# Routing in a two-layer decoder trunk: the choice of experts split between seven tiles and the last, block counts ahead of ranks, embedding projections moved

## What is computed

```python
a = rmsnorm(h)
y = concat(norm(sgu(a)), norm(conv_module(a)), norm(attention(a)))
h = h + y @ w_o                       # the output projection
m = rmsnorm(h)
glog = m @ wg + bg                    # 4 groups
elog = m @ we + be                    # 32 experts, 8 in a group
# the best group, in it the two best experts of each token
# tokens sorted by expert, in blocks that hold one expert each
h = h + sum over the 2 experts: weight * (silu(m @ w_gate[e]) * (m @ w_up[e])) @ w_down[e]
h = h + sigmoid(rmsnorm(h) @ ple_gate) * rmsnorm(p @ ple_proj)   # p: an embedding per token
```

## Time and profile before

| | |
|---|---|
| Time, median of 3 runs | 2171.34 us (2170.77 to 2174.62) |
| The profiled execution, span | 2165.7 us |
| PE busy | 1985.7 us, 92% |
| DVE busy | 1033.4 us, 48% |
| ACT busy | 638.2 us, 29% |
| POOL busy | 374.1 us, 17% |
| Output projection loop of layer 0 | 435 to 587 us |
| Routing until the first expert transposes | 587 to 627 us |
| Expert blocks | 627 to 949 us |
| Embedding stage | 949 to 1090 us |

### The profile page before, as it was taken

How to read it: one execution, slowest core, us unless ns; L and a number is a source line. 1 busy time by engine, 2 the same in 40 slices (tenths; PEclk the granted TensorE clock), 3 DMA queues, 4 the chain that set the end, 5 groups by cost and what they waited for, 6 DMA issues and landing times.

```text
span 2165.7 us, 34769 instructions
## 1 busy us (share of the span) xinstructions
PE 1985.7 (92%) x8952; PEld 1098.1 (51%) x8952; DVE 1033.4 (48%) x2327; ACT 638.2 (29%) x1521; POOL 374.1 (17%) x542
## 2 busy tenths in 40 slices
PE   6999789999969999989979997898999699999898
PEld 3555456655535545544435554666555354445443
DVE  3489867754341111125434897676543421111353
ACT  3333365522111111132133333555221111111321
POOL 2232100021012222210022221000210122222100
PEclk9999999999979999999989998999999799999999
DMA  7011241000389999965210112410003899999522
GB/s 252 15 29 29 55 160 30 26 20 30 133 322 393 389 382 375 389 233 202 83 29 15 29 29 60 155 30 26 20 30 136 313 389 384 373 378 370 178 96 97
DMA packets 122222, 361.97 MB, mean 167 GB/s; under 512 B 18853, under 2 KB 54005, under 8 KB 105220
## 3 DMA queue, kind: packets, MB, share of 16 engines
q1 hardware_dynamic: 105028, 318.74, 40.6%
q0 software_dynamic: 14784, 33.59, 4.2%
q10 hardware_dynamic: 2304, 8.39, 0.9%
HBM read 319.50 MB, written 59.51 MB: 175 GB/s over the span
## 4 chain that ended last, share of the span: by engine, by line
PE 76%; DMA 11%; DVE 5%; issue 4%; ACT 3%; SPq 1%; DVEq 0%; POOL 0%; ACTq 0%; POOLq 0%
PE ps L1806 30%; DMA region_c<-in_moe_w_up_dram 8%; PE ps L2169 7%; PE ps L1827 4%; PE ps L1969 4%; PE ps L2165 4%; PE ps L1985 4%; PE ps L2005 4%; PE ps L2190 4%; PE ps L1775 3%; PE ps L2184 2%; DMA region_a<-in_moe_w_up_dram 2%; PE ps L2150 2%; PE ps L1901 2%; PE ps L2091 2%
## 5 line engine op out<-in xcount | busy, mean ns | idle before, releaser
L1806 PE MATMUL ps<-region_b,region_c 128*128 128x512 f32 x1024 | 448.0, 593 | 2.8 <-DVE region_c L1271 2.7
L1806 PEld LDWEIGHTS ps<-region_b,region_c 128*128 128x128 f32 x1024 | 191.7, 190 | 226.9 <-issue 226.4
L1806 PE MATMUL ps<-region_a,region_c 128*128 128x512 f32 x512 | 224.3, 592 | 0.0
L1686 DVE SCALAR_TENSOR_TENSOR region_a<-region_a,ps 128x128 f32<-128x128 f32 x66 | 23.4, 354 | 385.5 <-ACT region_a L1134 385.5
L2169 PE MATMUL ps<-region_c,region_a 128*128 128x512 f32 x336 | 148.6, 595 | 14.1 <-DMA region_c<-in_moe_w_up_dram 13.9
L1806 PEld LDWEIGHTS ps<-region_a,region_c 128*128 128x128 f32 x512 | 96.5, 190 | 117.0 <-issue 117.0
L1969 PE MATMUL ps<-region_c 96*128 96x512 f32 (+3 forms) x384 | 146.6, 491 | 0.0
L1134 ACT ACTIVATE region_a<-ps 128x128 f32<-128x128 f32 x66 | 21.8, 331 | 363.1 <-PE ps L2169 242.4
L1466 DVE TENSOR_REDUCE neg_max<-ps 128x1 f32<-128x128 f32 (+7 forms) x128 | 96.9, 757 | 50.7 <-PE ps L1976 47.4
L1985 PE MATMUL ps<-ident,region_a 128*128 128x128 f32 x576 | 91.0, 285 | 26.5 <-ACT region_a L1066 25.0
L2169 PEld LDWEIGHTS ps<-region_c,region_a 128*128 128x128 f32 x336 | 62.1, 190 | 93.6 <-issue 93.6
(11 more groups left out here) (352 smaller groups left out, 3092.5 us busy)
## 6 DMA issues: line engine op xcount, KB each, us to landing
region_c<-in_moe_w_gate_dram SPq DMA_DIRECT2D x44, 1024.0 KB, 10.2
region_c<-in_moe_w_up_dram SPq DMA_DIRECT2D x44, 1024.0 KB, 17.1
region_c<-in_moe_w_down_dram SPq DMA_DIRECT2D x44, 1024.0 KB, 12.9
region_a<-in_moe_w_gate_dram SPq DMA_DIRECT2D x22, 1024.0 KB, 10.6
region_a<-in_moe_w_up_dram SPq DMA_DIRECT2D x22, 1024.0 KB, 17.4
region_a<-in_moe_w_down_dram SPq DMA_DIRECT2D x22, 1024.0 KB, 13.0
region_c<-choice_outputs SPq DMA_DIRECT2D x32, 512.0 KB, 4.5
qk_heads<-gains SPq DMA_DIRECT2D x32, 384.0 KB, 4.0
```

Source lines behind the costliest of these rows:

```text
L1806: ins = mm(dst, lhsT[:, k, :], w[:, k, a:b], start=(k == 0), stop=(k == KD - 1))
```

## The change

PE's list in the output projection loop becomes another: the second half of the projection is cut in two, `w_hi(0)` and `w_hi(1)` (8 instructions each), with `conv_turn` and `g_main` between them; `turn_p` (transposes of the embedding inputs) comes one step earlier; and `project(0)` stands ahead of the last tile's `turn_m`. The group and the best expert of tiles 0 to 6 are chosen on DVE inside the last pass of the loop, ahead of `w_main(1)` (`first_of_most`), the second-best after the evacuation of the last tile's m (`second_of_most`); the last tile has a chain of its own on 32 columns. PE counts and ranks seven tiles first, then the last, and signals `counts` ahead of `ranks`. The block counts are rounded in float with fewer operations, and PE forms the sum for the pairs. `key_half` and `key` come behind `owner_i`, the group softmax (`g_exp`, `g_sum`, `g_w`) behind the block lists. `project(1)` moves behind `owners`.

```diff
-                    if isinstance(t, int) and t == TILES - 1:
+                    def go():
                         for k in range(EARLY_P // 2):
                             act.wait_ge(*PT_pe.after(l, f"pair{k}"))
...
-
-                lag_loop(act, [(-1, norm_m), (2, later(norm(1))), (1, later(turn(1))), (-1, p_turned), (-1, turn_m), (3, late(c_tanh)), (3, late(c_yT_evac))])
-                act.wait_ge(*K_vec.after(l, "g_diff"))
-                nc.scalar.activation(rs(1, TILES, NG), rs(0, TILES, NG), ACT.Exp).then_inc(*K_act.next("g_exp"))
+                    guarded(act, i > PAIRS - 2, go)
+
+                lag_loop(act, [(-1, norm_m), (2, later(norm(1))), (1, later(turn(1))), (0, p_turned, 1), (-1, turn_m), (3, late(c_tanh)), (3, late(c_yT_evac))])
...
                 act.wait_ge(*FX.square.before(24 * l + 2 * TILES))
                 embedded(0)
-                embedded(1)
-                act.wait_ge(*K_vec.after(l, "e_diff"))
+                act.wait_ge(*K_vec.after(l, "g_diff"))
+                nc.scalar.activation(gs(1, TILES), gs(0, TILES), ACT.Exp).then_inc(*K_act.next("g_exp"))
                 nc.scalar.activation(rs(9, 2, TILES)[:, 1], rs(9, 2, TILES)[:, 0], ACT.Exp).then_inc(*K_act.next("e_exp"))
-                for t in range(2, EARLY_P):
+                for t in range(1, EARLY_P):
...
+            link0(v.tensor_scalar(iota64[:, :], iota[:, 0:NE], 1.0 / 64, None, ALU.mult), "parts")
...
-                lag_loop(v, [(-1, norm_m), (2, later(norm(1))), (1, later(turn(1))), (3, late(conv_centre)), (-1, turn_m), (0, w_main(0)),
-                             (3, late(conv_scale)), (3, late(conv_silu)), (0, w_main(1)), (-1, g_main), (3, late(conv_out))])
...
+                def largest_of_most(src, top, where, hot, n):
+                    link(v.tensor_reduce(top[:, 0:MOST], src[:, 0:MOST], AX.X, ALU.max), f"m{n}_most")
+                    link(v.tensor_tensor(cand[:, 0:MOST], src[:, 0:MOST], bc(top[:, 0:MOST], NE), ALU.is_lt), f"lt{n}_most")
+                    link(v.tensor_tensor(cand[:, 0:MOST], cand[:, 0:MOST], row(NE), ALU.add), f"cand{n}_most")
+                    link(v.tensor_reduce(where[:, 0:MOST], cand[:, 0:MOST], AX.X, ALU.min), f"i{n}_most")
+                    link(v.tensor_tensor(hot[:, 0:MOST], row(NE), bc(where[:, 0:MOST], NE), ALU.is_equal), f"hot{n}_most")
...
+                def first_of_most():
...
+                    link(v.tensor_reduce(sm(0)[:, 0:MOST], gl_[:, 0:MOST], AX.X, ALU.max), "g_max_most")
+                    link(v.tensor_tensor(below, gl_[:, 0:MOST], bc(sm(0)[:, 0:MOST], NG), ALU.is_lt), "g_lt_most")
+                    link(v.tensor_tensor(ahead, below, row(NG), ALU.add), "g_cand_most")
+                    link(v.tensor_reduce(sm(3)[:, 0:MOST], ahead, AX.X, ALU.min), "g_first_most")
+                    link(v.tensor_tensor(other, row(NG), bc(sm(3)[:, 0:MOST], NG), ALU.not_equal), "g_ne_most")
+                    link(v.scalar_tensor_tensor(e_in[:, 0:MOST].rearrange("p t (g e) -> p t g e", g=NG),
+                                                other.unsqueeze(3).to_broadcast([P, MOST, NG, EPG]), -BIG,
+                                                el[:, 0:MOST].rearrange("p t (g e) -> p t g e", g=NG), ALU.mult, ALU.add), "e_in_most")
+                    largest_of_most(e_in, sm(4), sm(5), hot1, 1)
...
+                def second_of_most():
+                    link(v.scalar_tensor_tensor(rest[:, 0:MOST], hot1[:, 0:MOST], -2 * BIG, e_in[:, 0:MOST], ALU.mult, ALU.add), "rest_most")
+                    largest_of_most(rest, sm(6), sm(7), hot2, 2)
+                    link(v.tensor_tensor(picked_b[:, 0:MOST], hot1[:, 0:MOST], hot2[:, 0:MOST], ALU.add), "picked_most")
+
+                def first(t, u, i):
+                    guarded(v, i > PAIRS - 2, first_of_most)
+
+                def second_choice(t, u, i):
+                    if isinstance(t, int) and t == TILES - 1:
+                        second_of_most()
+
+                lag_loop(v, [(-1, norm_m), (2, later(norm(1))), (1, later(turn(1))), (3, late(conv_centre)), (-1, turn_m), (-1, second_choice),
+                             (0, w_main(0)), (3, late(conv_scale)), (3, late(conv_silu)), (-1, g_main), (0, first, 1), (0, w_main(1)),
+                             (3, late(conv_out))])
...
+                def largest_of_last(src, top, where, hot, n):
+                    link(v.tensor_reduce(top[:, LAST], last(src), AX.X, ALU.max), f"m{n}_last")
+                    link(v.scalar_tensor_tensor(last(cand), last(src), top[:, LAST], iota64[:, :], ALU.is_lt, ALU.add), f"cand{n}_last")
+                    link(v.tensor_reduce(where[:, LAST], last(cand), AX.X, ALU.min), f"i{n}_last")
+                    link(v.tensor_scalar(last(hot), iota64[:, :], where[:, LAST], None, ALU.is_equal), f"hot{n}_last")
...
+                link(v.tensor_reduce(sm(0)[:, LAST], last(gl_), AX.X, ALU.max), "g_max_last")
+                link(v.scalar_tensor_tensor(last(gs(3, TILES)), last(gl_), sm(0)[:, LAST], iota64[:, 0:NG], ALU.is_lt, ALU.add), "g_cand_last")
+                link(v.tensor_reduce(sm(3)[:, LAST], last(gs(3, TILES)), AX.X, ALU.min), "g_first_last")
+                link(v.tensor_scalar(far, iota64[:, 0:NG], sm(3)[:, LAST], -BIG, ALU.not_equal, ALU.mult), "g_far_last")
+                link(v.tensor_tensor(last(e_in).rearrange("p (g e) -> p g e", g=NG), last(el).rearrange("p (g e) -> p g e", g=NG),
+                                     far.unsqueeze(2).to_broadcast([P, NG, EPG]), ALU.add), "e_in_last")
+                largest_of_last(e_in, sm(4), sm(5), hot1, 1)
+                link(v.scalar_tensor_tensor(last(rest), last(hot1), -2 * BIG, last(e_in), ALU.mult, ALU.add), "rest_last")
+                largest_of_last(rest, sm(6), sm(7), hot2, 2)
+                link(v.tensor_tensor(last(picked_b), last(hot1), last(hot2), ALU.add), "picked_last")
...
-                link(v.tensor_tensor(e2[:, 0], sm(6), sm(4), ALU.subtract), "e_diff")
...
-                v.wait_ge(*K_pe.after(l, "ranks"))
-                link(v.tensor_copy(cnt[:, 0:1], ps[0:NE, 6, 0:1]), "cnt_i")
-                link(v.tensor_scalar(cnt[:, 1:2], cnt[:, 0:1], HALF - 1, None, ALU.add), "cnt_full")
-                link(v.tensor_scalar(cnt[:, 2:3], cnt[:, 0:1], P - 1, None, ALU.add), "cnt_all")
-                link(v.tensor_scalar(cnt[:, 3:5], cnt[:, 1:3], 7, None, ALU.logical_shift_right), "cnt_nb")
-                link(v.tensor_copy(nb_f[:, 0:2], cnt[:, 3:5]), "nb_f")
-                link(v.tensor_tensor(nb_f[:, 2:3], nb_f[:, 1:2], nb_f[:, 0:1], ALU.subtract), "n_half")
-                link(v.tensor_scalar(nb_cols[0:NE, 0], ones_b[0:NE, :], nb_f[:, 0:1], None, ALU.mult), "col_full")
-                link(v.tensor_scalar(nb_cols[0:NE, 1], ones_b[0:NE, :], nb_f[:, 2:3], None, ALU.mult), "col_half")
+                v.tensor_tensor(e2[:, 0], sm(6), sm(4), ALU.subtract).then_inc(*K_vec.next("e_diff"))
+                v.tensor_tensor(gs(0, TILES), gl_, sm(0).unsqueeze(2).to_broadcast([P, TILES, NG]), ALU.subtract).then_inc(*K_vec.next("g_diff"))
+
+                nb_f = at(cin1, 264, 2)[0:NE]
+                v.wait_ge(*K_pe.after(l, "counts"))
+                v.tensor_scalar(nb_f[:, 0:1], ps[0:NE, 6, 0:1], (HALF - 1 - (P - 1) / 2) / P, ROUND, ALU.add, ALU.add)
+                link(v.tensor_scalar(nb_f[:, 1:2], ps[0:NE, 6, 0:1], (P - 1) / 2 / P, ROUND, ALU.add, ALU.add), "cnt_nb")
+                v.tensor_scalar(nb_cols[0:NE, 0], ones_b[0:NE, :], nb_f[:, 0:1], ROUND, ALU.mult, ALU.subtract).then_inc(*K_vec.next("col_full"))
+                link(v.tensor_scalar(nb_cols[0:NE, 1], ones_b[0:NE, :], nb_f[:, 1:2], nb_f[:, 0:1], ALU.mult, ALU.subtract), "col_half")
 
...
                 cols = at(cin1, 64, 3)[0:NE]
-                g = [at(cin1, 80 + k, 1) for k in range(5)]
-                both, quarter, whole, n_pairs, shift = g
-                link(v.tensor_copy(ends, bank(6, 64, 64 + 4 * NE).rearrange("p (a e) -> p a e", a=4)), "start_f")
-                link(v.tensor_copy(cols[:, 0:2], ps[0:NE, 6, 192:194]), "cols_f")
-                link(v.tensor_tensor(both, n_full, n_half, ALU.add), "both")
-                link(v.tensor_scalar(quarter, both, 0.5, 0.25, ALU.mult, ALU.add), "quarter")
-                link(v.tensor_scalar(whole, quarter, ROUND, None, ALU.add), "whole")
+                whole, n_pairs, shift = (at(cin1, 80 + k, 1) for k in range(3))
+                v.tensor_copy(ends, bank(6, 64, 64 + 4 * NE).rearrange("p (a e) -> p a e", a=4)).then_inc(*K_vec.next("start_f"))
...
+                link(v.tensor_reduce(sm(1), gs(1, TILES), AX.X, ALU.add), "g_sum")
+                link(v.reciprocal(sm(2), sm(1)), "g_w")
...
-                def w_half(k):
+                def w_lo(t, u, i):
+                    turned(1, t)
+                    pe.wait_ge(*W_vec.after(TILES * l + t - 1, "lo"))
+                    product(bank(2), aT[u] if t else aT_first, w_o, 0, 512).then_inc(*W_pe.next("lo"))
+
```

(56 more changed lines are left out.)

92 lines of the change are left out of this document (42 added, 50 removed).

## The result

The changed kernel takes 2201.99 us (median of 4 runs, 2196.18 to 2206.81) against 2171.06 (4 runs, 2165.98 to 2174.62): a ratio of 1.0141 with an interval of 1.0116 to 1.0166. It is 31 us slower. The forecast of 2181.7 had the direction right. The size lies outside its range, 11 us above 2191.

The account below looks back on a forecast made before the run. PE was taken to bound the loop, DVE's chain of small operations the routing. Per layer 11.2 lost less 6.0 gained, twice, is +10.4 us: span 2176.1, median 5.6 above it, 2181.7 us; range 2173 to 2191.

Parts of the forecast that it names:

- Part 1: Output projection loop: PE waits for c_silu ahead of conv_turn, 2.19 us in four steps, 3.07 in one; 11.2 us per layer.
- rival B: The loop's ten waits also cool PE's clock; three or four events give +8, 2190 us; chance 0.10.
- the sum: Both layers: 11.2 us lost in the loop less 6.0 gained in the routing, +5.2 per layer, +10.4 us in all.
- Part 2: Last tile: project(0) fills PE's wait, last router product takes 1.9 at full clock, routing starts 2 us later.
- Part 3: Routing: shorter DVE chain, counts 5.0 us earlier, owner_i 6.9, 6.0 per layer at the gather; projections last to arrive.
- Part 4: Expert blocks: DMA gets only some 3 us of the lead, but its slack absorbs this, so 6.0 stays.
- rival C: Routing gains only 3 us per layer because of DMA or the clock: 2187.7 us; chance 0.14.

Follow-up runs that it names:

- e3: The changed kernel with products that nobody reads put ahead of conv_turn, about as long as the waits: 2186.22 us, ratio 1.0064.
- e7: e1 with the embedding projections where they were before the change, 0 and 1 ahead of the counts, 2 and 3 behind owners: 2177.36 us, ratio 1.0019.
- e1: The changed kernel with conv_turn put back behind all of the second half, g_main ahead of w_hi(1) only for tile 6: 2164.06 us, ratio 0.9959.
- e5: e1 with project(1) right after the last router product, ahead of the counts, and all ranks behind owners: 2165.44 us, ratio 0.9972.
- e8: e1 with products that nobody reads in three PE waits around the last tile, ahead of project(0) and of the counts: 2165.74 us, ratio 0.9968.
- e2: The kernel before with only the loop's new order, conv_turn and g_main between the halves of w_hi, routing unchanged: 2213.85 us, ratio 1.0187.

## Why the prediction was right and wrong

**Part 1 was right about the waits.** Place, count, releaser and size all stand: 2.19 forecast and 2.02 idle in four steps, 3.07 and 2.89 in one. A step with an even clock is 20.80 long, as forecast, 2.23 more than before. The chain kept its length: `conv_turn` starts 6.70 behind `conv_back` (489.19 to 495.89), and I had 6.72. I had counted the wait from the distance to the next start (3.43 for eight instructions), where the profile counts it from their modelled end (3.60). In sum the lateness is 11.4 us per layer, against a forecast of 11.2. e3 shows it alone, with the clock left at 0.99. The rule on PE's order that part 1 takes from the Trainium skill, page "TensorE: Matmul & The Clock Gate", stands there in section "Step-by-step: what each phase is for" and not in the one named; the trace agrees, since nothing of `w_hi(1)` moved into the wait.

**The step that failed is rival B's term, left out of the sum and mis-sized.** I gave it a chance of 0.10 and "three or four events" at 1.7 to 3.4 us, +8 in all. The sum held nothing for it. In the profiled execution the falls behind the waits cost 20 us (of 5.9 and 17.7 us of longer busy time; the rest is the 0.2 per step and the slow first product), and in the median of the runs 16.7. Two things went wrong. The count: seven of ten waits were followed by a fall, in layer 1 every one, not three or four. And five of the seven were 6.7 us of half clock and cost 3.4, the upper end of my price. With the sum's own 10.4, 16.7 more gives 2198, near the median.

The evidence that I set against B was one 1.83 stall in the expert blocks, with full pace behind it. It is still true, and did not carry over. A single stall says that a fall does not have to follow. It says nothing on a wait that comes back in each step: of the four waits of 2.0 in layer 0, two passed without a fall and two did not. I had a row for the other side, the 2.80 wait with 0.50 behind it, nearer in kind to ten waits of 2 to 3, and I should have priced the sum by it: ten times its 1.7 is 17. That this is so near is luck in part, since fewer waits were followed by a fall and most of the falls cost more. The Trainium skill, page "TensorE: Matmul & The Clock Gate", section "HAM oscillation — how this bites in real kernels", describes a loop in which a wait for data brings the throttle back at each turn. I had cited only the page's earlier section. The changed kernel beside e3 agrees with that: 24.15 a step against 20.80.

**Part 2 held.** `project(0)` lay in the wait, at full clock (3.70; 3.43 forecast), and the last product took 1.95 (1.9). The logits came 2.2 later than before, 2 forecast. e7 bears the mechanism out: without `project(0)` in that wait the last product took 3.60. That `project(0)` itself ran at full clock was luck: behind the same wait of 1.91 it took 5.39 in e1 and in e5.

**Part 3 held nearly to the tenth.** The last tile's chain took 3.6 (3.6 forecast), the counts came 4.7 earlier (5.0), `owner_i` 7.1 (6.9), the gather 6.1 (6.0). The lists follow right behind the three projections, so that those are the last to arrive, as forecast. My sum did not say which edit carries this gain; e7 shows that without the projections' move nothing of it is left.

**Part 4 was too sure.** Of the 6.1 at the gather's issue 5.1 reached the first expert transposes in layer 0 (66.05 to 60.98 from the last `w_lo`) and 5.8 in layer 1. The blocks then took 1.0 and 0.5 more, so that 4.1 and 5.4 were left. I had 6.0, with rival C at 3.0 for a loss to DMA. In layer 0 the gather's landing took longer, from issue to transposes 7.60 in place of 6.54. SP's third block's load came 0.9 behind the first expert transposes, where it had stood 3.2 ahead. SP's queue:

```profile
641.97 0.34 SPq L652 DMA_DIRECT2D region_c<-in_moe_w_gate_dram  x1
```

That fits my reading that it waits for the stored embeddings, which now come later. But the blocks' time does not follow this load. In e7 it came 4.1 ahead and layer 0's blocks took 326.19; in e8 it came 0.9 behind and they took 324.21. In e5 it came 3.7 ahead, with 324.16 in layer 0 but 317.47 in layer 1, more than the changed kernel's. What makes the blocks differ by 1 or 2 us from kernel to kernel is open.

**The median and the span.** I set the median 5.6 above the span. The profiled execution's own time lies 1.7 above its span (2206.81 and 2205.1). The rest of the 5.6 was the difference between one execution and another.

In the end the sign came from the wait that was read in the trace. The size came in part from that and in part from a clock term which I had seen, named, and priced by the mildest row.

## What to carry to other kernels

Where PE is the bound, count the work between the start of a chain on another engine and the PE instruction that waits for it, and keep it longer than the chain; here half of a 6.9 us product moved behind the wait uncovered 2.0 us in each step. A short wait that recurs in each step of a dense loop must be priced twice, once for the idle time and once for the granted clock, which in layer 1 here cost more than the waits themselves (15 us against 11). If such a wait can't be avoided, compare with its place filled by unread products: that separates the two, and was faster than the wait here.

## What the runs showed of the hardware

Waits of 2.0 us, one in each 20.8 us step and with PE dense between them, brought the granted clock from 1.00 to the half level (0.52 over 7 us) for up to 6.7 us per step; one wait of 1.16 in each layer still did so, for about half as long; with the waits filled by matmuls it did not happen behind any of them. The same wait in the same program did it in one step and not in the next, and in the changed kernel in two steps of layer 0 and in all five of layer 1. In e2, where only the loop's order was changed, it was three in layer 0 and two in layer 1. A single fall can't be read from the time of a run: it costs 1.7 or 3.4 us, and the runs of the changed kernel lie between 2196 and 2207 us, those of the kernel before between 2166 and 2175. What decides between a fall and none, apart from the idle time, no run here shows.
